# An encoder layer's attention on one core: the softmax multiply by the inverse sum done by ScalarE in place of VectorE

## What is computed

```
s = jnp.einsum('bqhd,bkhd->bhqk', qb, k).astype(jnp.float32) * scale
s = s + jnp.transpose(cqb, (0, 2, 1))[..., None] - c_kT[:, :, None, :]
s = jnp.where((k_pos[None, :] <= pb[:, None])[None, None], s, NEG_INF)
p = jax.nn.softmax(s, axis=-1)
return jnp.einsum('bhqk,bkhd->bqhd', p.astype(v.dtype), v)
```

## Time and profile before

| what | value |
|---|---|
| median of three runs | 2045.76 us |
| the profiled execution, its own time | 2043.6 us |
| its span | 2041.6 us |
| TensorE matmul / weight load busy | 1917.4 us (94%) / 1853.4 us (91%) |
| VectorE busy | 1216.8 us (60%) |
| ScalarE busy | 442.7 us (22%) |
| GpSimd busy | 777.2 us (38%) |
| units of the attention stage | about 325 to 633 us of the span |

### The profile page before, as it was taken

The page is one execution under the profiler, slowest core; times in us unless marked ns, Lnnn a source line. Parts: engine busy times, 40 slices in busy tenths (PEclk is TensorE's granted clock), DMA queues, the critical chain, the costliest instruction groups (busy, mean ns, idle before and its releaser), DMA issues. The chain is left out here.

```text
span 2041.6 us, 29305 instructions
## 1 busy us (share of the span) xinstructions
PE 1917.4 (94%) x11561; PEld 1853.4 (91%) x11561; DVE 1216.8 (60%) x1906; ACT 442.7 (22%) x805; POOL 777.2 (38%) x389
## 2 busy tenths in 40 slices
PE   7999997888988999999997989999999999999984
PEld 6999996777888899989997989999999999999973
DVE  6788634666764554543563487556557655755746
ACT  4210103444542122131010132111111111111122
POOL 4434332212123764413223356435524633652500
PEclk8999998998999999999998999999999999999986
DMA  8635638364443343265433112111101201211102
GB/s 258 199 105 153 223 110 211 96 169 122 103 122 134 82 102 88 66 180 197 139 118 129 41 42 63 31 35 57 51 21 51 62 30 31 62 41 31 51 2 88
DMA packets 208697, 198.92 MB, mean 97 GB/s; under 512 B 48641, under 2 KB 186733, under 8 KB 208034
## 3 DMA queue, kind: packets, MB, share of 16 engines
q1 hardware_dynamic: 189026, 156.56, 27.0%
q10 hardware_dynamic: 19584, 41.17, 5.9%
HBM read 135.69 MB, written 57.54 MB: 95 GB/s over the span
## 5 line engine op out<-in xcount | busy, mean ns | idle before, releaser
L150 PE MATMUL ffn_ps<-act_hi,w_hi 128*128 128x364 f32 (+1 forms) x1248 | 412.4, 330 | 17.9 <-DVEq L1144 11.6
L150 PE MATMUL ffn_ps<-act_hi,w_lo 128*128 128x364 f32 (+1 forms) x1248 | 411.7, 330 | 0.0
L150 PE MATMUL ffn_ps<-act_lo,w_hi 128*128 128x364 f32 (+1 forms) x1248 | 411.6, 330 | 0.0
L150 PEld LDWEIGHTS ffn_ps<-act_hi,w_hi 128*128 128x128 f32 x1248 | 235.5, 189 | 19.0 <-DVEq L1144 11.9
L150 PEld LDWEIGHTS ffn_ps<-act_lo,w_hi 128*128 128x128 f32 x1248 | 235.3, 189 | 0.2
L150 PEld LDWEIGHTS ffn_ps<-act_hi,w_lo 128*128 128x128 f32 x1248 | 235.4, 189 | 0.0
L1200 DVE SCALAR_TENSOR_TENSOR conv<-up_raw,cw,conv 128x1090 f32<-128x1090 f32 x88 | 184.1, 2093 | 66.5 <-ACT up_raw L1108 37.3
L150 PE MATMUL mix_ps<-act_hi,w_hi 128*128 128x364 f32 (+1 forms) x552 | 186.9, 339 | 7.3 <-PEq L80 5.5
L934 POOL CAST w_hi<-w_raw 128x1024 fp32r<-128x1024 f32 x44 | 48.3, 1099 | 362.5 <-PE ffn_ps L150 351.1
L1275 POOL TENSOR_TENSOR w_raw<-w_raw,gain 128x1024 f32<-128x1024 f32 x24 | 47.8, 1993 | 362.5 <-PE gate_ps L150 254.4
L150 PE MATMUL mix_ps<-act_lo,w_hi 128*128 128x364 f32 (+1 forms) x552 | 182.4, 330 | 0.0
(11 more groups left out here) (328 smaller groups left out, 4069.6 us busy)
## 6 DMA issues: line engine op xcount, KB each, us to landing
w_raw<-in_w_up SPq DMA_DIRECT2D x44, 512.0 KB, 3.8
w_raw<-in_w_in SPq DMA_DIRECT2D x42, 512.0 KB, 4.6
gate<-gate_scratch ACTq DMA_DIRECT2D x24, 544.0 KB, 3.7
w_raw<-in_w_down SPq DMA_DIRECT2D x22, 512.0 KB, 3.5
w_raw<-in_w_branch SPq DMA_DIRECT2D x12, 512.0 KB, 4.2
gate_scratch<-gate_out ACTq DMA_DIRECT2D x11, 544.0 KB, 2.8
kh<-kh_scratch SPq DMA_DIRECT2D x16, 336.0 KB, 7.2
kl<-kl_scratch SPq DMA_DIRECT2D x16, 336.0 KB, 8.1
```

What stands on the lines that cost most here:

```text
L150: mm = pe.matmul(out, w(k), x(k)[:, c0:c0 + cn], start=first and k == ks[0] and n == 0, stop=last and k == ks[-1] and n == 2)
```

## The change

The scalar engine's function `normalise` multiplies `prob` by `inv` with an `activation` of kind Copy whose scale is the column `inv`. The vector engine's function, now `invert`, keeps the reciprocal. The new call stands first in ScalarE's loop. The semaphores are the same: `inv_done` from VectorE, `norm_done` now from ScalarE.

```
             for n in range(N + 3):
+                if n < N:
+                    normalise(n)
                 if 1 <= n <= N:
                     prob_high(n - 1)
...
+            def normalise(n):
+                nq, _, nk, _ = extent(n)
+                x = n % 3
+                act.wait_ge(inv_done, n + 1)
+                act.activation(prob[0:nq, x, 0:nk], prob[0:nq, x, 0:nk], ACT.Copy, scale=inv[0:nq, x:x + 1]).then_inc(norm_done, 1)
...
-            def normalise(n):
-                nq, _, nk, _ = extent(n)
+            def invert(n):
+                nq = extent(n)[0]
                 x = n % 3
                 dve.wait_ge(exp_done, n + 1)
                 dve.reciprocal(inv[0:nq, x:x + 1], total[0:nq, x:x + 1]).then_inc(inv_done, 1)
-                dve.wait_ge(inv_done, n + 1)
-                dve.tensor_scalar(prob[0:nq, x, 0:nk], prob[0:nq, x, 0:nk], inv[0:nq, x:x + 1], None,
-                                  ALU.mult).then_inc(norm_done, 1)
...
             for n in range(N + 3):
                 if n < N:
-                    normalise(n)
+                    invert(n)
```

## The result

| | before | with the change |
|---|---|---|
| median | 2045.51 us (4 runs) | 2066.12 us (4 runs) |
| lowest to highest | 2044.78 to 2048.79 | 2062.30 to 2068.28 |
| span of the profiled execution | 2041.6 us | 2064.9 us |

The ratio is 1.0096, 95% interval 1.0077 to 1.0115: slower by 16 to 24 us, beyond the 0.2% that a measurement tells. The forecast was 2065 (2050 to 2083).

A forecast was written before the change was run, and what follows sets the result against it. TensorE was taken as the bound of the attention stage, with holes from waits ended by VectorE. Terms 10.6 + 7.5 + 4.6 - 6 + 3 gave +20 us on 2043.6 or 2045.76, so 2065 us, range 2050 to 2083.

The forecast's parts named there:

- term (2): Value product ahead of a gate piece, behind one iteration without (15 places): longer wait for the low half, 7.5 us.
- term (1): Iterations without a gate piece behind another without (13): longer chain from row maximum to row maximum, 10.6 us.
- term (3): TensorE's turn in the attention stage waits for its own unit's multiply: 4.6 us together.
- Term (5): Gain in the attention stage from GpSimd's stalls of VectorE's multiply going away: -6 us, between 0 and -10.1.
- Term (6): Granted clock over the attention stage: more waits lower it, up to 6 us more, partly inside waits, counted +3 us.
- A: Whole kernel faster because GpSimd's stalls decide: at most -10 us, 2036 us; chance 8%.
- B: ScalarE's pass and copy in series on all 43 iterations without a piece: 42 us, net +36, 2081 us; chance 14%.
- C: Lengthening in the attention stage half hidden, no clock loss, all stalls back: +7 us, 2052 us; chance 20%.
- D: Nothing measurable, gate pieces hide all: 2046 us; chance 6%.
- Term (4): ScalarE's two output stores before the next multiply fit beside Exp and Tanh: nothing; at worst 0.5 us in some 10 places.
- the forecast's sign that the stretched neighbours are gone: Sign of being right: in the profile after the change, GpSimd's stretched neighbours are gone; no size given.

The follow-up runs named there:

- 7: Kernel before, with GpSimd's three instructions cut to two columns of each later weight tile in the attention stage: 2030.58 us, ratio 0.992.
- 10: Kernel before, with ScalarE's high copy made to wait for VectorE's multiply and GpSimd's passes cut to two columns: 2050.56 us, ratio 1.002.
- 8: Changed kernel, with GpSimd's passes cut to two columns of each later weight tile in the attention stage: 2065.96 us, ratio 1.0103.
- experiment 2: Kernel before, with one wait added: ScalarE waits for VectorE's multiply of the next unit ahead of the high copy: 2061.86 us, ratio 1.0086.
- the thin pair (3 and 4): Multiply cut to one column, on ScalarE in the changed kernel: 2041.97 us; on VectorE in the kernel before: 2027.47 us.
- experiment 5: Changed kernel, with ScalarE's multiply right behind its own Exp and VectorE's reciprocal ahead of the next unit's row maximum: 2035.29 us, ratio 0.9946.

## Why the prediction was right, and which sizes were wrong

The ratios of 7, 10, 8 and the change, each against the kernel before, take the change apart; each step is uncertain by some 3 to 5 us, and holds what the step did to the clock as well as to the waits:

| step | from, to | share |
|---|---|---|
| GpSimd's passes no longer felt | 1 to 0.992 (7) | -16 us |
| the copy waits for the multiply | 0.992 to 1.002 (10) | +20 us |
| the multiply is ScalarE's, and longer | 1.002 to 1.0103 (8) | +17 us |
| GpSimd's passes in the changed kernel | 1.0103 to 1.0096 | -1 us |
| sum | | +20 us |

In another order the shares shift a little: the wait costs 18 us with GpSimd's passes in place (experiment 2), and cutting them then gives back some 13 (experiment 2 to 10).

**The mechanism** held: the multiply in front of the high copy, behind the maximum of the unit after; the low half waiting on the copy (91.8 us for 7.1). The busy times came as forecast, VectorE 165.5 for 165, ScalarE 198 for 204.

**The price of the new pass** was right: 1.149 us at 1024 columns and 0.509 at 256, Exp's 1.145 and 0.499 of the earlier trace rows and not the plain copy's. The estimate by the Trainium skill, "ScalarE: Activation LUTs", section "What ACT_TABLE_LOAD costs", was 1.13 us; these rows agree.

**Terms (1) to (3)**, together 22.7 us for queue and pass, stand against 37 us in the table, 20 for the queue where I had about 11 and 17 for the pass where I had 12. But they were sums of waits, and the 37 hold the clock. TensorE's waits and its busy time (325 us to its last turn), in us, in the three runs without GpSimd's passes:

| TensorE waits for | 7 | 10 | 8 |
|---|---|---|---|
| the row maximum | 17.9 | 20.8 | 19.5 |
| the low half, for the value product | 7.4 | 13.6 | 13.9 |
| the multiply, for the turn | 1.9 | 2.0 | 14.0 |
| the output's sum | 2.8 | 3.9 | 2.3 |
| all four | 30.0 | 40.3 | 49.7 |
| TensorE busy | 264.0 | 270.4 | 275.0 |

From 7 to 8 the waits grow by 19.7 us, near the 22.7. How they divide is not as I had it: the value product's grows by 6.5 (term (2): 7.5), the row maximum's by 1.6 where term (1) had 10.6, and the turn's by 12.1 where term (3) had 4.6. The queue (7 to 10) shows mostly in the value product's wait, the multiply's move to ScalarE (10 to 8) almost only in the turn's: the turn waits for a multiply that ends later. A delay in one iteration can show at either of the two, so the sum of (1) and (3), 15.2 for 13.7, is surer than each.

**Term (5)**, the stalls, was too small: -6 for -16 (-13 to -20). TensorE's waits fell by 8.6 us in the seventh experiment, and its busy time up to the last turn by 4.7. The term's bound of -10.1 was the excess of the 15 stretched multiplies alone; it left out the 4.3 us of the stretched L766, and the clock.

**Term (6)**, the clock, is the term that was most mis-sized. I had +3 us. With the change TensorE is busy 10.9 us longer with the same matmuls (279.6 for 268.7). The granted clock says the same: 0.96 over 307 us before, a loss of 12 us by my way of counting, and 0.93 over 329 us with the change, a loss of 23. With the 10.8 us more of waits this makes the 21.4 us by which the stage is longer. In 553 to 563 us, for one, TensorE had 6.97 of 10 us busy and a mean clock of 0.81, between its two levels of 1.2 and 2.4 GHz (0.5 and 1.0). In the thin pair (3 and 4) the clock moved with hardly any change in the waits, and the eighth, as slow as the change, shows 0.95 in one execution. No run holds the clock fixed; so what a wait costs through the clock is read from the traces, not shown. The prediction's remark that a stretch with "the two waits of the earlier trace rows" kept 1.00 mixes two places: the earlier trace rows shows one wait of 1.48 us, at 374 us; the stretch 569 to 577 us holds another of 1.48 (at 572.13) and one of 0.96.

The total came out within 1 us by luck: the waits rose by 10.8 us where (1) to (3) and (5) make 16.7, and the clock cost about 11 where I had 3. It is a right account of the direction and of what the high copy waits for, not of the sizes.

**The rivals.** A (faster by the stalls) had a stronger case than 8%: its gain is 16 us, and with another place in the queue, experiment 5, it wins. B (the chain in all 43 iterations) named a loss of 42 us, nearer to the 37 than my 22.7; but it was a sum of waits, and those rose by 19.7, which fits the forecast's view that the iterations behind a piece catch up; no run tested that by itself. C and D fell. The rule of the Trainium skill, "ScalarE: Activation LUTs", section "Rules for kernel authors", to keep a plain multiply on VectorE, gave the right side here, but the fifth experiment breaks it with a gain of 11 us.

**Small things.** Term (4) read the stores as fitting beside other passes. They do not always: in the changed kernel the multiply stands idle 1.8 us in four places, 7.2 us in all, while ScalarE's queue issues a gate's store and two of the output. Such waits were there before, in front of the high copy (21.0 us in 15). What they cost the end, no run shows.

## What to carry to other kernels

When work moves to an idle engine, ask first which instruction it will stand in front of, and what the moved one waits for: here the same instructions gave 2066, 2046 or 2035 us by their order in the queues (in the last, the reciprocal's place on VectorE changed too). What won here was to put the moved work right behind the step that feeds it on the same engine, and to make its other input as early as that. Price a stall by removing its cause once, and look for every instruction it touches: here 14.3 us of stretched VectorE time, of which I had seen 10.1, cost 16 us (13 to 20) of the end in the kernel before, through waits (8.6) and through the clock, and nothing that can be told in the changed one. And count the waits and the busy time of the bounding engine apart: half of this loss was TensorE doing the same work for longer.

## What the runs showed of the hardware that I had not expected

GpSimd's passes hold up more on VectorE than the multiply. The output's low half (two inputs in SBUF) is stretched too, in both kernels, so the forecast's sign that the stretched neighbours are gone held for the multiply only. Before, two instances of 64x256 took 2.57 us (one of them is shown with experiment 7); the mean with GpSimd's passes cut is 0.41. In the changed kernel the one of 64 columns takes 1.86 us beside a GpSimd pass that ends with it (375.24 + 2.38 = 377.62; 375.83 + 1.86 = 377.69):

```profile
375.24 2.38 POOL L1284 TENSOR_TENSOR w_lo<-w_raw,w_hi 128x1024 fp32r<-128x1024 f32 x1
...
375.83 1.86 DVE L771 TENSOR_TENSOR o_lo<-o_sum,o_hi 64x64 fp32r<-64x64 f32 x1
```

In the kernel before, this shape's mean was 0.209 us. The Trainium skill, "SBUF — State Buffer", section "Who interferes with whom", states this for VectorE instructions with two SBUF inputs against GpSimd ones that read SBUF; the trace agrees. Cutting GpSimd's passes takes 4.3 us off this instruction in the kernel before and 4.9 in the changed one, where that gained nothing: there VectorE waits for ScalarE anyway (91.8 us).

ScalarE's multiply is not stretched in the same place: the one that starts at 376.24 us, inside the GpSimd pass above, takes 0.72 us for 512 columns, the mean of its shape, and the longest of all 72 takes 1.152.
